# Up-products of three feed-forward stages: high and low half of the activation in one 512-column pass

## The reference, cut to what matters

```python
D_MODEL = 1024; SEQ = 256; D_FF = 2816; CONV_W = 3

def conv_ffn(h, w_up, conv_w, conv_b, w_down):
    L = h.shape[1]
    u = h @ w_up
    r = CONV_W // 2
    up = jnp.pad(u, ((0, 0), (r, r), (0, 0)))
    acc = conv_b
    for j in range(CONV_W):
        acc = acc + up[:, j:j + L] * conv_w[j]
    a, g = jnp.split(acc, 2, axis=-1)
    return (jax.nn.silu(g) * a) @ w_down

def conv_ffn_2(h, norm_g, w_up, conv_w, w_down):
    xn = rms_norm_2(h, norm_g)
    u = causal_dwconv(xn @ w_up, conv_w)
    g, val = u[..., :D_FF], u[..., D_FF:]
    return (jax.nn.silu(g) * val) @ w_down
```

## Time and profile before

| what | value |
|---|---|
| median of 3 runs | 1420.56 us (1420.47 to 1421.38) |
| the profiled execution, its own time | 1417.93 us |
| its span, first to last instruction | 1416.1 us |
| mean granted clock of PE | 0.958 |
| PE busy | 1327.5 us, 94% of the span, 9656 matmuls |
| DVE busy | 739.8 us, 52% |
| ACT busy | 631.8 us, 45% |
| POOL busy | 688.2 us, 49% |

### The profile page before, as it was taken

One profiled execution on the slowest core, in us unless ns is written; L12 is line 12 of the kernel. 1 busy time (PEld: TensorE's weight loads), 2 busy tenths in 40 slices (PEclk: granted clock), 3 DMA queues, 4 the chain that ended last, 5 costly groups with the idle time before them and its releaser, 6 DMA issues.

```text
span 1416.1 us, 25587 instructions
## 1 busy us (share of the span) xinstructions
PE 1327.5 (94%) x9656; PEld 1197.0 (85%) x9656; DVE 739.8 (52%) x1363; ACT 631.8 (45%) x1084; POOL 688.2 (49%) x296
## 2 busy tenths in 40 slices
PE   5879989979999989999898998899999999899999
PEld 0657878957769989999886676899999999899999
DVE  3530025459552267776515454167777533577775
ACT  2422243325445465555543333455555554655553
POOL 1443462214225845556684400435557597555564
PEclk9999999979999999999999859899999999999999
DMA  9676441213113635555553300235556465355552
GB/s 375 216 265 243 166 134 58 60 30 105 46 60 119 181 124 177 186 179 197 169 176 94 117 1 0 90 112 184 182 186 210 136 195 189 108 178 178 178 184 99
DMA packets 57742, 208.50 MB, mean 147 GB/s; under 512 B 6576, under 2 KB 7600, under 8 KB 57408
## 3 DMA queue, kind: packets, MB, share of 16 engines
q1 hardware_dynamic: 57168, 205.55, 43.5%
q0 software_dynamic: 496, 1.87, 0.3%
HBM read 206.35 MB, written 1.05 MB: 146 GB/s over the span
## 4 chain that ended last, share of the span: by engine, by line
PE 87%; DVE 4%; DMA 3%; ACT 3%; issue 2%; POOL 1%; SPq 0%; DVEq 0%; ACTq 0%
PE ps L438 22%; PE ps L439 21%; PE ps L440 21%; DMA raw<-in_stream 3%; PE ps L663 2%; PE ps L468 2%; PE ps L470 2%; PE ps L471 2%; PE ps L501 1%; PE ps L751 1%; PE ps L876 1%; PE ps L536 1%; PE ps L725 1%; PE ps L705 1%; PE ps L645 1%
## 5 line engine op out<-in xcount | busy, mean ns | idle before, releaser
L294 POOL TENSOR_TENSOR wlo<-raw,whi 128x1024 fp32r<-128x1024 f32 x284 | 682.4, 2419 | 689.5 <-ACT whi L1056 688.0
L438 PE MATMUL ps<-Hh,whi 128*128 128x256 f32 (+2 forms) x1976 | 579.7, 293 | 27.0 <-DVE arena L1892 6.6
L439 PE MATMUL ps<-Hl,whi 128*128 128x256 f32 (+2 forms) x1976 | 570.4, 289 | 0.0
L440 PE MATMUL ps<-Hh,wlo 128*128 128x256 f32 (+2 forms) x1976 | 569.9, 288 | 0.0
L438 PEld LDWEIGHTS ps<-Hh,whi 128*128 128x128 f32 (+1 forms) x1976 | 383.4, 194 | 48.3 <-issue 20.8
L1056 ACT ACTIVATE whi<-raw 128x1024 fp32r<-128x1024 f32 x338 | 352.9, 1052 | 151.6 <-DMA raw<-in_stream 69.5
L439 PEld LDWEIGHTS ps<-Hl,whi 128*128 128x128 f32 (+1 forms) x1976 | 384.1, 194 | 2.7
L440 PEld LDWEIGHTS ps<-Hh,wlo 128*128 128x128 f32 (+1 forms) x1976 | 383.6, 194 | 2.7
L1836 DVE SCALAR_TENSOR_TENSOR arena<-ps,sm,arena 128x255 f32<-128x255 f32 (+1 forms) x264 | 127.2, 482 | 105.8 <-ACT arena L1302 98.6
L438 PE MATMUL ps<-dh,whi 128*128 128x256 f32 x592 | 168.4, 285 | 5.7 <-DVE wlo L1812 3.0
L439 PE MATMUL ps<-dl,whi 128*128 128x256 f32 x592 | 168.2, 284 | 0.0
(11 more groups left out here) (291 smaller groups left out, 1322.1 us busy)
## 6 DMA issues: line engine op xcount, KB each, us to landing
raw<-in_stream SPq DMA_DIRECT2D x386, 512.0 KB, 4.3
X<-in_xc SPq DMA_DIRECT2D x2, 1024.0 KB, 10.6
out_y<-X SPq DMA_DIRECT2D x8, 128.0 KB, 1.9
kx<-in_const POOLq DMA_DIRECT2D x1, 512.0 KB, 7.1
arena<-in_wgate POOLq DMA_DIRECT2D x1, 400.0 KB, 9.1
params<-in_params POOLq DMA_DIRECT2D x1, 372.0 KB, 7.0
k<-in_const POOLq DMA_DIRECT2D x1, 256.0 KB, 5.0
kx<-in_const POOLq DMA_DIRECT2D x1, 256.0 KB, 4.4
```

What stands on the lines that cost most here:

```text
L294: pool.tensor_tensor(wlo[:, slot, :], raw[:, rslot, :], whi[:, slot, :].bitcast(f32), ALU.subtract).then_inc(rest_done[0], 1)
L438: pe.matmul(out, lh, rh, start=start, stop=False, skip_group_check=True)
L439: pe.matmul(out, lh, rl, start=False, stop=False, skip_group_check=True)
L440: return pe.matmul(out, ll, rh, start=False, stop=stop, skip_group_check=True)
```

## The change

The up-products of the three feed-forward stages use a new helper, `product_c`. The tiles `Hh` and `Hl` become the two halves of one tile `H`, and for each chunk one matmul with the high weights reads both halves, 512 columns, into the whole bank: columns 0 to 255 get high weight by high activation, columns 256 to 511 get high weight by low activation. A second matmul of 256 columns adds low weight by high activation to the first half. ACT then copies the second half of the bank to the new tile `LOW` (part of `arena`; semaphore `low_out`), and DVE adds it to the first half in place (semaphore `joined`). The ACT instruction order changes too: for each j, first the copy, then the weight split, then the centre tap. The copies of the taps are made by ACT, after `dh`, in place of DVE. The down-products and all other stages stay as they are.

```diff
@@ -128,8 +128,8 @@
         whi = sb("whi", [P, RING, 1024], f32r)
         wlo = sb("wlo", [P, RING, 1024], f32r)
         X = sb("X", [P, KC, 2 * T])
-        Hh = sb("Hh", [P, KC, 2 * T], f32r)
-        Hl = sb("Hl", [P, KC, 2 * T], f32r)
+        H = sb("H", [P, 2, KC, 2 * T], f32r)
+        Hh, Hl = H[:, 0, :, :], H[:, 1, :, :]
         dh = sb("dh", [P, 2, T], f32r)
         dl = sb("dl", [P, 2, T], f32r)
         AR = sb("arena", [P, A_END])
@@ -197,6 +197,7 @@
         mod_rows = ar(A_MO + 512, 512)
         ROWJ = sb("junk", [P, T], mybir.dt.bfloat16)
         TC = [[work[:, 512 * s + 256 * j:512 * s + 256 * j + 256] for j in range(2)] for s in range(2)]
+        LOW = [[work[:, 2048 + 512 * s + 256 * j:2304 + 512 * s + 256 * j] for j in range(2)] for s in range(2)]
         mixC = [work[:, 256 * s:256 * s + 256] for s in range(2)]
         mixT = [work[:, 1024 + 256 * s:1280 + 256 * s] for s in range(2)]
 
...
@@ -450,6 +451,18 @@
                     if norm is not None:
                         pe.wait_ge(S["hl_done"], HU[norm] + (2 * k + 2 if norm == 0 else k + 1))
                     mm = mm3(out, *w(s, k), Hh[:, k, c0:c0 + n], Hl[:, k, c0:c0 + n], k == 0, k == KC - 1)
+                mm.then_inc(blk_done, 1)
+
+            def product_c(s, bank, norm=None):
+
+                both = PS[:, bank, :].rearrange("p (a t) -> p a t", a=2)
+                for k in range(KC):
+                    if norm is not None:
+                        pe.wait_ge(S["hl_done"], HU[norm] + k + 1)
+                    wh_, wl_ = w(s, k)
+                    pe.matmul(both, wh_, H[:, :, k, 0:T], start=k == 0, stop=False, skip_group_check=True)
+                    mm = pe.matmul(PS[:, bank, 0:T], wl_, Hh[:, k, 0:T], start=False, stop=k == KC - 1,
+                                   skip_group_check=True)
                 mm.then_inc(blk_done, 1)
 
             def product_n(s, width, k0, at, norm=None):
@@ -828,7 +841,7 @@
                             pe.wait_ge(S["down_lo"], v(base + i - 1, 2))
                         elif i >= 2:
                             pe.wait_ge(S["conv"], v(4 * NF * nf + 4 * (i - 2) + 2 * j + 2, 8))
-                        product_t(s, PS[:, 4 + 2 * (i % 2) + j, 0:T], 0, T, norm if (i, j) == (0, 0) else None)
+                        product_c(s, 4 + 2 * (i % 2) + j, norm if (i, j) == (0, 0) else None)
                         if (i, j) == (0, 0) and norm >= LATE:
                             sumsq(norm)
                     if 1 <= i <= NF - held_of(f):
@@ -1275,8 +1288,15 @@
 
             def ffn(f):
                 nf, base = FFN_STARTS.index(f), DOWN[f]
+                cw = FFP[f][0]
+                copies = NF * nf
                 act.preload_act_table_set("silu_and_others")
                 splits_upto(f + 5)
+
+                def copy_taps(i, m=None):
+                    lo = PC[cw][0] + 8 * i
+                    src = PR[:, lo:lo + 8] if m is None else PR[:, bass.ds(lo + 16 * m, 8)]
+                    act.activation(cwb[:, i % 2, :], src, ACT.Copy).then_inc(S["cw_copy"], 1)
 
                 def step(i, m=None):
 
@@ -1291,8 +1311,12 @@
                     slot = i % 2
                     for j in range(2):
                         tc = TC[slot][j]
+                        act.wait_ge(blk_done, v(up_block(f, 2, NF, i, j) + 1, RING))
+                        act.activation(LOW[slot][j], PS[:, 4 + 2 * slot + j, T:2 * T], ACT.Copy)\
+                           .then_inc(S["low_out"], 1)
+                        splits(up_block(f, 2, NF, i, j))
                         if f == S_FFN1:
-                            act.wait_ge(blk_done, v(up_block(f, 2, NF, i, j) + 1, RING))
+                            act.wait_ge(S["joined"], v(2 * i + j + 1, 4))
                         else:
                             act.wait_ge(S["scaled"], v(2 * NF * (nf - 1) + 2 * i + j + 1, 4))
                         act.wait_ge(S["cw_copy"], v(NF * nf + i + 1, 2))
@@ -1301,7 +1325,6 @@
                         bias = cwb[:, slot, 6 + j:7 + j] if f == S_FFN1 else 0.0
                         act.activation(tc, PS[:, 4 + 2 * slot + j, 0:T], ACT.Identity, bias=bias,
                                        scale=cwb[:, slot, 3 * j:3 * j + 1]).then_inc(S["centre"], 1)
-                        splits(up_block(f, 2, NF, i, j))
 
                     gate = 1 if f == S_FFN1 else 0
                     act.wait_ge(S["conv"], v(4 * NF * nf + 4 * i + 2 * gate + 2, 8))
@@ -1311,9 +1334,13 @@
                     if 2 <= i < NF - 2:
                         act.wait_ge(blk_done, v(down_block(f, 2, NF, i - 2) + 1, RING))
                     act.activation(held_pair(f, NF, i)[0], gated, ACT.Copy).then_inc(S["down_hi"], 1)
+                    if m is not None or i + 2 < NF:
+                        copy_taps(i + 2, m)
                     if 1 <= i <= NF - held_of(f):
                         splits(down_block(f, 2, NF, i - 1))
 
+                copy_taps(0)
+                copy_taps(1)
                 step(0)
                 step(1)
                 with act.Fori(0, LOOPS[f]) as m:
@@ -1801,11 +1828,6 @@
                 gate = 1 if f == S_FFN1 else 0
                 copies = NF * nf
 
-                def copy_taps(i, m=None):
-                    lo = PC[cw][0] + 8 * i
-                    src = PR[:, lo:lo + 8] if m is None else PR[:, bass.ds(lo + 16 * m, 8)]
-                    dve.tensor_copy(cwb[:, i % 2, :], src).then_inc(S["cw_copy"], 1)
-
                 def rest(s, m=None):
 
                     dve.wait_ge(hi_done, s + 1 if m is None else s + 1 + RING * m)
@@ -1821,8 +1843,10 @@
                         rest(down_block(f, 2, NF, i - 1), m)
                     for j in range(2):
                         u, tc = PS[:, 4 + 2 * slot + j, :], TC[slot][j]
+                        dve.wait_ge(S["low_out"], v(2 * NF * nf + 2 * i + j + 1, 4))
+                        dve.tensor_tensor(u[:, 0:T], u[:, 0:T], LOW[slot][j], ALU.add).then_inc(S["joined"], 1)
                         if f != S_FFN1:
-                            dve.wait_ge(blk_done, v(up_block(f, 2, NF, i, j) + 1, RING))
+                            dve.wait_ge(S["joined"], v(2 * NF * nf + 2 * i + j + 1, 4))
                             dve.tensor_tensor(u[:, 0:T], u[:, 0:T], n_r[:, 0:T], ALU.mult).then_inc(S["scaled"], 1)
                         dve.wait_ge(S["centre"], v(2 * NF * nf + 2 * i + j + 1, 4))
                         if f == S_FFN1:
@@ -1837,8 +1861,6 @@
                                                      cwb[:, slot, 3 * j + 1 + n:3 * j + 2 + n], tc[:, lo:hi],
                                                      ALU.mult, ALU.add).then_inc(S["conv"], 1)
                     dve.wait_ge(S["conv"], v(4 * NF * nf + 4 * i + 4, 8))
-                    if m is not None or i + 2 < NF:
-                        copy_taps(i + 2, m)
                     dve.wait_ge(S["silu_done"], v(NF * nf + i + 1, 2))
                     h = PS[:, 4 + 2 * slot + gate, 0:T]
                     dve.tensor_tensor(h, h, TC[slot][1 - gate], ALU.mult).then_inc(S["h_ff"], 1)
@@ -1846,8 +1868,6 @@
                     hi, lo = held_pair(f, NF, i)
                     dve.tensor_tensor(lo, h, hi.bitcast(f32), ALU.subtract).then_inc(S["down_lo"], 1)
 
-                copy_taps(0)
-                copy_taps(1)
                 step(0)
                 step(1)
                 with dve.Fori(0, LOOPS[f]) as m:
```

More of the change, by code:

```diff
@@ L223, in build @@
             "row_act", "ctx_exp", "lat_exp", "ml_sq", "ml_act", "att_exp", "sink_act", "recip_out", "sig_done", "t_hi",
-            "down_hi", "centre", "silu_done", "f_act", "sb_l", "sb_w", "fox_exp", "t2_hi", "cu_c", "mix_t",
+            "down_hi", "low_out", "centre", "silu_done", "f_act", "sb_l", "sb_w", "fox_exp", "t2_hi", "cu_c", "mix_t",
             "x_ready", "x_unit", "newton", "h32_done", "hl_done", "small", "mod_ready", "evac_v", "gate_add", "gate_lf",
@@ L228, in build @@
             "ml_norm", "qk_fin", "mask_ready", "att_max", "pt_done", "sink_sum", "recip", "att_out", "ml_m32", "t_lo",
-            "mix_y", "down_lo", "scaled", "conv", "h_ff", "cw_copy", "f_add", "f_lf", "cf_ready", "sb_sp", "sb_spm",
+            "mix_y", "down_lo", "joined", "scaled", "conv", "h_ff", "cw_copy", "f_add", "f_lf", "cf_ready", "sb_sp", "sb_spm",
             "sb_arg", "sb_wm", "sb_out", "fox_max", "fox_pt", "fox_out", "t2_lo", "mix_cu", "fin", "wg_lo",
```

## The result

The changed kernel took 1436.32 us (median of 4 runs, 1435.06 to 1436.84), the kernel before 1420.97 (4 runs, 1420.47 to 1422.20): a ratio of 1.0105, 95% interval 1.0088 to 1.0123. It was 15 us slower where 7.5 us less were forecast, outside the range.

The account below looks back on a forecast made before the run. PE was taken to set the pace in the middle of the feed-forward stages. Terms -13.0 + 3.2 + 1.7 + 0.6 = -7.5 us took the median of 1420.56 to 1413.1 us, range 1408.0 to 1419.5.

Parts of the forecast that it names:

- Merged pass, -13.0: Up-products of the feed-forward stages: 512-column pass at 226.5 ns replaces two of 120.0, 0.108 us saved on each of 120.
- Starts, +3.2: First down-product of each feed-forward stage: longer bare ACT and DVE chain adds 1.1, 1.15 and 0.9 us.
- Clock behind the longer waits, +1.7: After the longer waits at the three stage starts: one loss to half clock in all, 1.7 us; ends 0 and 5.1.
- Ends, +0.6: Last steps of the second and third feed-forward stages: DVE falls behind, last result 0.3 us late in each.
- the likeliest case: The main forecast, 70%: 1413.1 us, said to reach by itself from 1409.5 to 1417.5 us.
- DVE and ACT as the bound: Rival, 14%: in the stages' middle DVE needs 8.66 us a step against PE's 8.424; 1425.2 us.
- the side that I expected: Middle of the stages: DVE's weight split meets no POOL split, so 7.6 us a step is enough for DVE.
- The merged pass at 237.5: Rival, 6%: in the up-products the two-piece read costs nearly two matmuls, 237.5 ns; +3.1 us, 1423.7 us.
- No loss at starts and ends: Rival, 8%: the removed long tap copies pay for the new pieces at starts and ends; -14.3 us, 1406.3 us.
- Theory A: From the experiments: second attention stage's 18.9 us come from PE's granted clock, which hangs on how work falls in time.

Follow-up runs that it names:

- a_near: Changed kernel with each chunk's two halves 2 KB apart instead of 16 KB; seven of ten runs 1414.1 to 1420.7 us, three 1433.5 to 1437.9.
- a_contig: Changed kernel with the wide pass reading 512 unbroken columns of the weight slot, so up-products are not computed; one run, 1414.12 us.
- s_fill: Changed kernel plus 24 matmuls ahead of the second attention stage's forgetting heads, eight wide passes sorted before eight narrow; mean 1427.31 us.
- b_d10: Kernel before with 10 more matmuls early in the second attention stage; one run, 1437.71 us.
- t_fill: Kernel before with tap copies moved to ACT, plus 24 matmuls ahead of the second attention stage's forgetting heads; mean 1420.62 us.
- b_pass: Changed kernel with the tap copies back on DVE, leaving merged pass and joining alone; four runs, 1438.4 to 1443.7 us.
- b_taps: Kernel before with only the tap copies moved from DVE to ACT; five of ten runs 1414.2 to 1420.4 us, five 1434.9 to 1436.0.
- t_fill12: Kernel before with tap copies on ACT and 12 matmuls ahead of the forgetting heads; ten of twelve runs 1418.0 to 1422.5 us, two at 1439.9.
- the shifted kernels: Kernel before and changed kernel, each with 10 or 20 more matmuls early in the second attention stage; one run each, 1437.71, 1439.69, 1436.52, 1437.02 us.
- a_fill: Changed kernel with 24 matmuls more ahead of the second attention stage's forgetting heads; twelve runs, mean 1421.87 us.

## Why the prediction was wrong

**What failed is the step from the changed stages to the whole.** The sum took every stretch outside the three stages as it stood in one profiled execution of before, and the range was built from costs inside them. Of the granted clock it only asked what a longer wait at the three starts might do. The same clock decides 19 us in the second attention stage, in code that the change leaves alone, and before's own execution was the short one of two. A row for it could be had: the trace of before shows that stage at 0.50 up to 851 us and at 1.00 behind, with a wait of 1.2 us at the seam. None of my rivals asked what a shift does there. The first comparison, four long against four short, showed a ratio of 1.0105 that mixes the two forms; over all runs changed is long far more often (9 of 16 against 7 of 105), so the loss on average is real, but the time is not lost in the stages that I priced.

**The terms of the sum**, from the stage lengths and rows of the changed kernel:

- *Merged pass, -13.0.* Mis-sized by half. 353.1 ns a pair against 360.0: 6.9 ns by 960 pairs, -6.6 us. The direction was right. The measured 6.9 lies between the forecast's 13.5 and the 2.5 ns that follow from the formula of the Trainium skill (TensorE: Matmul & The Clock Gate, Back-to-back issue gap), which the section gives for isolated matmuls and not for a stream with a weight load before each; the trace agrees with neither. The row of wide matmuls behind wide ones did not stand for wide behind narrow. a_near and a_contig exclude the two places of the read; s_fill gets 3.7 of the 6.6 missing ns back by sorting, so the turns account for about half. The rest is open.
- *Starts, +3.2.* First down-products measured from the table load: 11.39, 9.49 and 11.39 us against 10.62, 8.49 and 10.60: +0.8, +1.0, +0.8, in all +2.6. Right, a little large.
- *Clock behind the longer waits, +1.7.* Zero. The waits of 1.83 and 2.15 us were not followed by a fall (1.00 from 956 to 958 us), and behind the third, 4.04 us, the clock was down as long as behind the 2.96 us of before. But this term turns out to be a coin as well: b_d10 has before's third stage with the same wait of 2.96 us and no fall behind it, and lasts 192.67 us there, against 194.1 in before:
```profile
1255.00:1257.00 2.00, 2.00 (x19) 2.00 (x18) 1.35 (x4) 1.48 (x3) 1.38 (x1) 1.00 0.83 297
```
So about 1.5 us of before's third stage hang on the clock.
- *Ends, +0.6.* Measured 0.4: a wait of 0.36 us at the last pair of the first stage, where I had expected none, and none in the others.
- *Missed, +1.4.* Behind the second stage DVE's first low half of the norm takes 2.20 us, against 0.83 before: it starts while POOL still works on a split that ACT now gives it later.
```profile
1131.19 2.20 DVE L1816 SCALAR_TENSOR_TENSOR H<-X,params,H 128x256 fp32r<-128x256 f32 x1 [0.83 <-ACT H L1278]
```
That POOL's split (1128.33 on) stretches it was read from the timeline, not tried.

The sum of these, -2.2, agrees with the table: -3.7 in the three stages, +1.4 behind, -2.3. Direct measurements: -1.0 (+-1.3) with the seam filled, and -0.33% (-0.17 to -0.49), 4.7 us (2.4 to 7), short against short. So with the long form out of play the three readings are 1.0, 2.2 and 4.7 us less, with the forecast's sign and short of its 7.5; the interval of the first includes no gain at all.

One slip in the sum as recorded: with the ends of its terms, the likeliest case reaches from 1409.2 to 1418.3 us, not from 1409.5 to 1417.5. Both lie inside the stated range, so nothing hangs on it.

**Of the parts**, the tap copy alone is worth as much as the whole or more: -3.5 us by the stages, of which 1.5 are the clock of the third stage, and -2.2 (+-1.5) measured in t_fill. The merged pass with its low copy and addition then costs about 1 us on top by the traces (+1.2 (+-1.4) by the runs; 3.6 us with the tap copies still on DVE, by the stages of b_pass, a part of it clock). Against b_taps it saves 6.6 on PE and gives back 4.6 at the starts, where the copies and additions stand bare, 0.4 at an end, 1.4 behind the second stage, and the 1.5 of the clock. The prediction gave nearly all the gain to the merged pass.

**The rivals.** DVE and ACT as the bound: no; DVE waits for its first low copy 0.7 us in each step, and two steps take 17.06 us (1012.93 to 1029.98 between its weight splits), PE's pace. DVE's weight split took 1.22 us each time, the side that I expected. The merged pass at 237.5: no, some 233. No loss at starts and ends: no.

**Theory A** is shown as far as this: both forms exist in the kernel before and in the changed one, unedited; in every long execution that was profiled PE is at half clock through the forgetting heads, and in every short one it is not; and dense PE work at the seam removes the long form from changed and from b_taps. Open is which arrivals lead to it (how long before the end of PE's wait the clock rises does not sort them: 2.30 us in b_taps, which stayed up, 2.42 in t_fill12, which fell again), and why changed, b_taps and the shifted kernels arrive badly more often than before: the spread of the time up to the first stage from run to run (491 to 497 us to the first norm's table load in the profiled ones) is larger than the shifts that I made, 1.2 and 2.4 us.

## What to carry to other kernels

A stage whose granted clock comes out one way or the other from run to run is a coin that any change elsewhere tosses again: look for stretches at 0.50 that end by themselves, and price both forms before summing. Compare such kernels by stage lengths in the trace, or with the coin held fixed, and count the runs in each form; a median of four says which side came up. Test each part of a change alone: here, by the traces, the small one carried the gain and the large one gave its own back.

## What the runs showed of the hardware

- PE at half clock with busy share 100%: in before the stick-breaking heads kept PE busy 41 of 41 us in the records and the clock stayed at 0.50 from 809 to 850 us. Busy in the records does not mean that the clock comes back.
- With 24 matmuls of 128x256 at the seam the clock, once fallen, was back some 3 us later and read 1.00 for the next 26 us of the same code (a_fill); without them it stayed down for over 50 us (after). Short runs with 24, 12 and 6 such matmuls: 36 of 36, 10 of 12, 3 of 12 (kernels without sorted passes).
- Behind one and the same wait of 2.96 us the clock fell in before and not in b_d10: 1.5 us.
- Wide behind wide took 226.5 ns, wide and narrow in turn 353.1 ns a pair, 6.6 more than the two alone; eight wide and then eight narrow 349.4.
- An 8-column copy took DVE 0.30, 0.82 or 2.26 us in different steps and kernels, and ACT 0.20 us.
